# Mixer convolution split by taps, recurrence stages moved back, and new orders at the opening and at four changes of stage, in a two-block float32 transformer kernel

## The chip, the cores and the metric

One core of a Trainium2 chip runs the whole program. The metric is the device time of one execution in microseconds (us); lower is better. Matrix products run on TensorE (PE in the profile), elementwise work on VectorE (DVE) and ScalarE (ACT), loads of weights are issued by SyncE's queue (SP), a few loads and fills by GpSimd (POOL).

## What is computed

A sequence of 256 tokens of width 1024 in float32 goes through two blocks, nine stages in a row (`STAGES`): feed-forward, mixer, feed-forward, twice for the first block, then feed-forward, another mixer, feed-forward for the second.

```python
# first block, for l in range(2): norms modulated by mod = silu(c) @ ada_w + ada_b
x = x + 0.5*mod * swiglu(h)          # 1024 -> 2816 -> 1024
x = x + mod * mixer(h)               # dilated attention and a gated convolution
x = x + 0.5*mod * swiglu(h)
# second block
h = h + 0.5 * rms_norm(swiglu(rms_norm(h)))
h = h + rms_norm(mixer2(rms_norm(h)))
h = h + 0.5 * rms_norm(swiglu(rms_norm(h)))
# in mixer2:
xr = causal_conv(xr, conv_w, conv_b)                 # 4 taps
r, ig = sigmoid(xr @ wa + ba), sigmoid(xr @ wx + bx) # block-diagonal
a = exp(-8 * r * softplus(-lam)); u = sqrt(-expm1(2*log a)) * (ig * xr)
h_t = a_t * h_(t-1) + u_t                            # the recurrence
y_a = (h * gelu(xg)) @ w_lru_out                     # beside windowed attention y_b
```

## The kernel before

**Products.** Each float32 product is made of three: operands are split into a rounded high part and the rest (low). ScalarE writes the high part (`split`, L697, 1.9 us for a 1 MB unit of weights), VectorE subtracts for the low part (`split`, L1170, 2.29 us, or `low_part`, L1177, by halves), and TensorE does low x high, high x low, high x high (`mm3` L1774 to L1776, `tok3` L1781 to L1783). SyncE loads the units in the order of use into three slots `raw`; the load of unit n waits until the low part of unit n-3 is done. High and low parts have three slots more, and every fourth unit of a feed-forward goes to a fourth one (`w3`).

**Orders by hand.** Each engine has a program of its own, written in the order in which it shall work, with semaphores between them. An instruction that waits holds everything behind it on its engine.

**Opening.** Eight units of `ada_w` (named u0 to u7 here) make the scales and shifts of the first norm. TensorE takes u1, u3 and u6 (`ada_cols_of`, L2040), VectorE u0, u2, u4, u5 and u7 in this order (`ada_unit`, L1193 and L1196), each followed on TensorE by a sum over partitions (L2055). When all are done, VectorE's `mods` (L1214, L1217) makes gain and shift. The norm of a tile of 128 tokens is: sums of squares on ScalarE (`norm_x`, L715 to L727), `normed` on VectorE (L1247), eight transposes on TensorE (`turn_x`, L1852), then `apply` on ScalarE (L762, L768) and VectorE (`lows`, L1272; in the second tile also L1258, L1260). In the opening, tile 0 is normed just before u7 and turned before `ada_cols_of(6)`. Tile 1 is normed after the second unit's low part and turned in the midst of the first product, by `mid` in `up(0, 1, 0, s, ...)`.

**Feed-forward.** Eleven groups i: two units of gate and up weights (`up`), transposes of the hidden tile (`turn_h`, L1870), then the down product of the group before (`down`), whose operands are `cH` (ScalarE, `hidden`, L853) and `cL` (VectorE, `low`, L1394). On VectorE the order in group 1 is: one unit of `ada_w` where this stage has one (4.2 us), low part of unit 5, `low(0)`, low part of unit 6. At the start both engines split unit 3 and then do `silu` (L844, L847) and `mult` (L1387, L1390) of group 0.

**Changes.** Between stages `change` computes statistics, the residual and the next norm. After stages 5 and 7 (`BARE`) the transposes take `x` itself and the factor of the norm is applied later, in `silu` and `mult`; ScalarE's order is there: apply, split of unit 2, `next_stats` of both tiles, load of the Silu table. After stage 6 ScalarE does: statistics of the product for tile 0, the first half of them for tile 1 (`row_first`), statistics of the new `x` for tile 0, the second half for tile 1. `squared` counts these for VectorE.

**Second mixer (stage 7).** TensorE works in 28 half units hu of 24 products (0.12 us apart each). After two of three comes one `tick` of attention (scores L1936, transposes L1947, product with the values L1962), after the third nothing; in the middle of the third `chunk_T` (L1974) turns a pair of heads. Six half units, hu - 2 = 6j + i, serve chunk j of the recurrence: unit "c" (convolution input), "q" (queries), "g" (gate). VectorE does `conv2(j)` at i = 0: copy L1714, then four taps (L1720 once, L1727 three times, each in two halves), and only then the next tick's logits (L1456, L1459) and `otok` (L1477) of the tick before. ScalarE does exponentials in each tick (L902), and around them sigmoids (L1100, L1102), tanh and exp (L1110, L1111), sqrt (L1114), `gelu` (L1121) and the high part `cH` (L1117), changing its activation table whenever the set differs. VectorE's stages of `lru(j, k)`: k = 0 at i = 4, k = 1 at i = 5, k = 2 (product, scan L1699, product with gelu) at i = 1 of the next chunk, k = 3 (`cL`, L1707) at i = 2. TensorE's products of the gates (L2174, L2176) come after the tick at i = 2 and wait for all taps. The units after these, `tail`, end in the output projection; its first recurrent unit waits at L1774 for the last `cL`.

## Time and profile before

| what | value |
|---|---|
| median of 3 runs | 2119.05 us (2118.66 to 2120.47) |
| the profiled execution | 2119.83 us, span 2118.0 us |
| PE busy | 2065.3 us, 98% of the span |
| DVE busy | 1419.6 us, 67% |
| ACT busy | 1031.6 us, 49% |
| granted TensorE clock | 0.996 on average |
| chain that ended last | PE 84%, DVE 6%, ACT 5%, DMA 2%, issue 2% |

The profiled execution's own time is 1.8 us above its span, and 0.8 us above the median. TensorE is nearly always busy; each gap in its work is shown in the trace with the engine and the line that ended it.

### The profile page before, as it was taken

The numbers are of one execution on the slowest core, as the hardware profiler recorded it, in microseconds if no ns is written. First come the engines' busy times: TensorE is split into PE (matmuls) and PEld (weight loads), VectorE is DVE, ScalarE is ACT, GpSimd is POOL, SyncE is SP. The second block draws the span as 40 slices with busy tenths as digits, with TensorE's granted clock in tenths as the row PEclk, the third lists the DMA queues.
The fourth block names the chain that finished last, engine by engine and source line by source line (L and its number), as shares of the span: only waits on it lengthen the run. The fifth ranks groups of instructions, "written<-read, shape, count | busy, mean of one in ns | idle before, by whom it ended". The sixth has DMA issues, their size and how long they took to land.

```text
span 2118.0 us, 29720 instructions
## 1 busy us (share of the span) xinstructions
PE 2065.3 (98%) x12033; PEld 1811.1 (86%) x12033; DVE 1419.6 (67%) x1801; ACT 1031.6 (49%) x1278; POOL 36.5 (2%) x78
## 2 busy tenths in 40 slices
PE   6999999999999999999999999999999899899998
PEld 6788899999888878888999998887788788897887
DVE  5787677668777777767766786555555577656454
ACT  3543544444544363445454446444644569646443
POOL 0000000000000000000000000000000000000000
PEclk9999999999999999999999999999999999999999
DMA  9787698547687758758865585554656434456552
GB/s 298 251 272 250 199 298 253 130 133 253 229 267 251 249 170 285 243 195 270 280 173 142 176 291 194 194 179 150 227 180 195 131 126 134 158 181 203 187 196 80
DMA packets 355933, 438.11 MB, mean 207 GB/s; under 512 B 9571, under 2 KB 323371, under 8 KB 355796
## 3 DMA queue, kind: packets, MB, share of 16 engines
q1 hardware_dynamic: 350592, 420.51, 60.8%
q0 software_dynamic: 4160, 14.23, 3.1%
q8 instruction: 96, 1.57, 0.3%
q10 hardware_dynamic: 1044, 1.46, 0.2%
q14 instruction: 41, 0.34, 0.0%
HBM read 435.05 MB, written 1.11 MB: 206 GB/s over the span
## 4 chain that ended last, share of the span: by engine, by line
PE 84%; DVE 6%; ACT 5%; DMA 2%; issue 2%; DVEq 1%; SPq 0%; ACTq 0%
PE PC L1781 7%; PE PC L1783 7%; PE PC L1782 7%; PE PA L1781 6%; PE PA L1783 6%; PE PA L1782 6%; PE PB L1781 5%; PE PB L1783 5%; PE PB L1782 5%; PE PA L1774 5%; PE PA L1775 5%; PE PA L1776 5%; PE PC L1774 2%; PE PC L1776 2%; PE PC L1775 2%; DVE acc L1196 2%
## 5 line engine op out<-in xcount | busy, mean ns | idle before, releaser
L1170 DVE TENSOR_TENSOR lo<-raw,hi 128x2048 fp32r<-128x2048 f32 x275 | 628.8, 2289 | 229.7 <-ACT hi L697 229.1
L697 ACT ACTIVATE hi<-raw 128x2048 fp32r<-128x2048 f32 x277 | 529.0, 1911 | 264.0 <-PE PC L1783 130.3
L1774 PE MATMUL PA<-nl,hi 128*128 128x256 f32 x976 | 281.5, 288 | 1.0 <-ACT f L1090 0.9
L1775 PE MATMUL PA<-nh,lo 128*128 128x256 f32 x976 | 276.0, 283 | 0.0
L1776 PE MATMUL PA<-nh,hi 128*128 128x256 f32 x976 | 275.9, 283 | 0.0
L1196 DVE SCALAR_TENSOR_TENSOR acc<-raw,cs,acc 128x256 f32<-128x256 f32 x448 | 217.1, 485 | 34.0 <-issue 0.4
L1781 PE MATMUL PA<-hi,nl 128*128 128x512 f32 (+1 forms) x528 | 210.8, 399 | 10.7 <-DVE nl L1272 7.6
L1783 PE MATMUL PA<-hi,nh 128*128 128x512 f32 (+1 forms) x528 | 206.4, 391 | 0.0
L1782 PE MATMUL PA<-lo,nh 128*128 128x512 f32 (+1 forms) x528 | 205.9, 390 | 0.0
L1774 PEld LDWEIGHTS PA<-nl,hi 128*128 128x128 f32 x976 | 187.0, 192 | 2.8 <-issue 1.1
L1775 PEld LDWEIGHTS PA<-nh,lo 128*128 128x128 f32 x976 | 187.0, 192 | 0.3
L1776 PEld LDWEIGHTS PA<-nh,hi 128*128 128x128 f32 x976 | 186.9, 191 | 0.0
L1781 PE MATMUL PB<-hi,nl 128*128 128x512 f32 x400 | 157.5, 394 | 0.6 <-DVE nl L1272 0.6
L1783 PE MATMUL PB<-hi,nh 128*128 128x512 f32 x400 | 156.0, 390 | 0.0
L1782 PE MATMUL PB<-lo,nh 128*128 128x512 f32 x400 | 155.6, 389 | 0.0
L1170 DVE TENSOR_TENSOR w<-raw,w 128x2048 fp32r<-128x2048 f32 x51 | 116.8, 2289 | 55.6 <-ACT w L697 55.6
L1781 PE MATMUL PC<-hi,cL 128*128 128x512 f32 x384 | 151.2, 394 | 2.6 <-DVE cL L1394 2.6
L1783 PE MATMUL PC<-hi,cH 128*128 128x512 f32 x384 | 149.7, 390 | 0.0
L1782 PE MATMUL PC<-lo,cH 128*128 128x512 f32 x384 | 149.5, 389 | 0.0
L1781 PEld LDWEIGHTS PA<-hi,nl 128*128 128x128 f32 x528 | 100.8, 191 | 34.2 <-issue 9.3
L1783 PEld LDWEIGHTS PA<-hi,nh 128*128 128x128 f32 x528 | 100.9, 191 | 20.9
L697 ACT ACTIVATE w<-raw 128x2048 fp32r<-128x2048 f32 x51 | 97.4, 1910 | 43.3 <-PE PC L1783 43.3
(305 smaller groups left out, 3867.2 us busy)
## 6 DMA issues: line engine op xcount, KB each, us to landing
raw<-in_w_in SPq DMA_DIRECT2D x90, 1024.0 KB, 6.4
raw<-in_ada_w SPq DMA_DIRECT2D x66, 1024.0 KB, 7.2
raw<-in_ffn_w_gate SPq DMA_DIRECT2D x88, 512.0 KB, 4.1
raw<-in_ffn_w_up SPq DMA_DIRECT2D x88, 512.0 KB, 5.1
raw<-in_ffn_w_down SPq DMA_DIRECT2D x44, 1024.0 KB, 5.0
raw<-in_ffn_w SPq DMA_DIRECT2D x88, 512.0 KB, 4.8
raw<-in_ffn_w SPq DMA_DIRECT2D x22, 1024.0 KB, 4.9
raw<-in_w_o SPq DMA_DIRECT2D x12, 1024.0 KB, 6.3
```

The costliest lines, as they stand in the source:

```text
L697: A(parts_of(n)[0], raw[:, n % 3, :], ACT.Copy).then_inc(hi_done, 1)
L1170: V.tensor_tensor(l, raw[:, n % 3, :], h.bitcast(F32), ALU.subtract).then_inc(lo_done, 1)
L1196: i = V.scalar_tensor_tensor(o, w[:, k, :], cs[:, k:k + 1], o, ALU.mult, ALU.add)
L1774: MM(o, wh[:, c0:c0 + w], xl, start=first, stop=False, skip_group_check=True)
L1775: MM(o, wl[:, c0:c0 + w], xh, start=False, stop=False, skip_group_check=True)
L1776: return MM(o, wh[:, c0:c0 + w], xh, start=False, stop=last, skip_group_check=True)
L1781: MM(o, xl, wh[:, c0:c0 + w], start=first, stop=False, skip_group_check=True)
L1782: MM(o, xh, wl[:, c0:c0 + w], start=False, stop=False, skip_group_check=True)
L1783: return MM(o, xh, wh[:, c0:c0 + w], start=False, stop=last, skip_group_check=True)
```

## The change

The diff, with its context cut. In the opening, VectorE norms tile 0 ahead of u5 and tile 1 ahead of `mods`; TensorE turns tile 0 and takes u6 before the sum of u5, and turns tile 1 after the last sum, so that `mid` is gone there. In group 1 of each feed-forward `low(0)` goes ahead of the low part of unit 5. After stages 5 and 7 the split of unit 3 goes ahead of the statistics on ScalarE and ahead of the reciprocals on VectorE. After stage 6 the statistics of tile 0's new `x` go ahead of both halves of tile 1's. In stage 7 taps 2 and 3 go behind the next tick (i = 1), `lru` stage 2 from i = 1 to i = 2, stage 3 from i = 2 to i = 4, ScalarE's `gelu` from i = 4 to i = 5 and its high part `cH` from i = 1 to i = 3. No instruction that computes is added or taken out.

```diff
...
 
 def squared(s, t, h):
 
-    if (s, t) == (6, 1):
-        return 3 * STAT[("p", 6, 0)] + 3 + (6 if h else 1)
     return 3 * STAT[("p", s, t)] + (3 if h else 1)
 
 
...
                     final_stats(1)
                     apply(Aq, 1)
                     split(BASE[s + 1] + 2)
+                    split(BASE[s + 1] + 3)
                     next_stats(s, 0)
                     next_stats(s, 1)
                     A(spare[:, :], eps[:, 0:1], ACT.Silu)
                 elif s == 6:
                     row_std(*post_of(s, 0))
-                    row_first(*post_of(s, 1))
                     next_stats(s, 0)
-                    row_second(*post_of(s, 1))
+                    row_std(*post_of(s, 1))
                     apply(Aq, 0)
                     next_stats(s, 1)
                     apply(Aq, 1)
...
                     row_std(*post_of(s, 1))
                     apply(Aq, 1)
                     split(BASE[s + 1] + 2)
+                    split(BASE[s + 1] + 3)
                     next_stats(s, 0)
                     next_stats(s, 1)
                     A(spare[:, :], eps[:, 0:1], ACT.Silu)
...
                     act.wait_ge(hT_done, (fo * NG + i) * 2 + t + 1)
                     A(by_tile(hid(cH, i))[:, t], turned(i)[:, t], ACT.Copy).then_inc(hH_done, 1)
 
-                split(b + 3)
+                if s - 1 not in BARE:
+                    split(b + 3)
                 silu(0, 0)
                 silu(0, 1)
                 split(b + 4)
...
 
                 act.wait_ge(rg_mm, j + 1)
                 if j:
-                    act.wait_ge(lru_v, 6 * j)
+                    act.wait_ge(lru_v, 6 * j - 1)
                 for m in range(2):
                     c = 2 * j + m
                     A(ra[:, m * T:(m + 1) * T], RA[:, m * T:(m + 1) * T], ACT.Sigmoid,
...
                     tick(2, 32, 0, t, STEPS)
                 if c is not None:
                     chunk_T(8 + c, c, oH2)
+                if i == 5 and 0 <= j < 4:
+                    gelu(j)
                 if i == 3 and j >= 0:
                     recurrent_gates(j)
+                if i == 3 and 1 <= j < 4:
+                    lru(j - 1, 2)
                 if i == 0 and j >= 1:
                     lru(j - 1, 1)
                 if i == 4 and 0 <= j < 4:
                     lru(j, 0)
-                    gelu(j)
                 if hu % 2 == 0 and u >= 0:
                     after(b + 3 + u)
                     if SPREAD[u] == "q":
...
                     elif SPREAD[u] in ("ga", "gc"):
                         gate2(f1 if SPREAD[u] == "ga" else f2, SPREAD[u], 0, prod[1])
                     split(b + 6 + u)
-                if i == 1 and j >= 1:
+                if i == 1 and j == 4:
                     lru(j - 1, 2)
 
             def last_chunks():
...
                     final_norm(1)
                     apply(Aq, 1)
                     behind()
+                    split(BASE[s + 1] + 3)
                     recip(("n", Aq, 0))
                     recip(("n", Aq, 1))
                 elif s == 6:
...
                     add_postnorm(s, 1)
                     apply(Aq, 1)
                     behind()
+                    split(BASE[s + 1] + 3)
                     recip(("n", Aq, 0))
                     recip(("n", Aq, 1))
                 else:
...
                     V.tensor_tensor(by_tile(hid(cL, i))[:, t], turned(i)[:, t], by_tile(hid(cH, i))[:, t].bitcast(F32),
                                     ALU.subtract).then_inc(hL_done, 1)
 
-                split(b + 3)
+                if s - 1 not in BARE:
+                    split(b + 3)
                 mult(0, 0)
                 mult(0, 1)
                 split(b + 4)
...
                 for i in range(1, NG - 1):
                     if i > 1 or first is None:
                         ada(mid[i])
-                    split(b + 3 * i + 2)
+                    if i > 1:
+                        split(b + 3 * i + 2)
                     low(i - 1)
+                    if i == 1:
+                        split(b + 3 * i + 2)
                     if i == 1 and first is not None:
                         ada(mid[i])
                     split(b + 3 * i + 3)
...
                 if n == 2:
                     dve.wait_ge(rowsT, 1)
                     V.tensor_copy(vec[:, :], PA[:, 0:384]).then_inc(vec_done, 1)
-                if n == 4:
+                if n == 3:
                     normed(0, 0)
                 dve.wait_ge(raw_full[u] if u < 4 else ada_in[u - 4], 16)
                 ada_unit(u * UC, first_ada(u), ada_d)
+            normed(0, 1)
             mods(0)
             low_part(0, 0)
             lows(0, 0, (0, 1))
             low_part(0, 1)
             lows(0, 0, (2, 3))
             split(1)
-            normed(0, 1)
+            dve.drain()
             apply(0, 1)
             split(2)
 
...
                     V.tensor_scalar(xc[:, m * T:(m + 1) * T], cpad[:, m, 1:1 + T],
                                     vec[:, V_CONV2 + c:V_CONV2 + c + 1], vec[:, V_CONVB2 + c:V_CONVB2 + c + 1],
                                     ALU.mult, ALU.add)
-                for tap in (1, 2, 3):
+                taps2(j, (1,))
+
+            def taps2(j, taps):
+
+                for tap in taps:
                     dve.drain()
                     for m in range(2):
                         c = V_CONV2 + 8 * tap + 2 * j + m
                         i = V.scalar_tensor_tensor(xc[:, m * T:(m + 1) * T], cpad[:, m, 1 + tap:1 + tap + T],
                                                    vec[:, c:c + 1], xc[:, m * T:(m + 1) * T], ALU.mult, ALU.add)
-                i.then_inc(xc_done, 1)
+                if taps[-1] == 3:
+                    i.then_inc(xc_done, 1)
 
             for hu in range(2 * len(SPREAD)):
                 t, c, u = tick_of(hu), chunk_of(hu), (hu - 3) // 2
...
                     tick(2, 32, 0, t, 8, STEPS)
                 if i == 0 and 0 <= j < 4:
                     conv2(j, c)
+                if i == 1 and 0 <= j < 4:
+                    taps2(j, (2, 3))
+                if i == 4 and 1 <= j < 4:
+                    lru(j - 1, 3)
+                    dve.drain()
                 if i == 4 and 0 <= j < 4:
                     lru(j, 0)
                 if i == 5 and 0 <= j < 4:
                     lru(j, 1)
-                if i == 1 and j >= 1:
+                if i == 2 and 1 <= j < 4 or i == 1 and j == 4:
                     lru(j - 1, 2)
                 if i == 0 and j == 4 and c is not None:
                     chunk_T(8 + c, c, oH2, oL2)
...
                     split(b + 6 + u)
                 if i == 3 and c is not None:
                     chunk_T(8 + c, c, oH2, oL2)
-                if i == 2 and 1 <= j < 4:
-                    lru(j - 1, 3)
 
             def last_chunks():
                 split(b + 19)
...
                         m.then_inc(d_done, 1)
 
                 up(0, 0, 0, s)
-                up(0, 1, 0, s, lambda: turn_x(s, 1))
+                up(0, 1, 0, s, (lambda: turn_x(s, 1)) if s else None)
                 up(0, 0, 1, s)
                 up(0, 1, 1, s)
                 if first is not None:
...
                     rows_turned()
                 if n == 1:
                     ada_cols_of(3)
-                if n == 4:
+                if n == 3:
                     turn_x(0, 0)
                     ada_cols_of(6)
                 pe.wait_ge(ada_d, n + 1)
                 for c in (2 * u, 2 * u + 1):
                     i = MM(MOD[:, c:c + 1], acc[:, c * P:(c + 1) * P], ones[:, 0:1], start=True, stop=True)
             i.then_inc(mod_done, 1)
+            turn_x(0, 1)
 
             def bias_lines():
```

## Rows read from the trace of the kernel before

**Rows 1.** The page, its first line

```profile
span 2118.0 us, 29720 instructions
```

**Rows 2.** Timeline of PE, 0 to 62 us: start us, us, instruction, [idle before <-releaser]

```profile
31.66 1.01 PE L2055 MATMUL PB<-ones,acc 128*128 128x1 f32 x4 [3.58 <-DVE acc L1196]
32.54 1.95 PE L1852 MATMUL PC<-ident,xn_b 128*128 128x128 f32 x8
34.28 6.83 PE L2040 MATMUL PB<-cs,early 128*128 128x1 f32 x32
...
44.59 0.76 PE L1781 MATMUL PA<-hi,nl 128*128 128x512 f32 x1 [2.63 <-DVE nl L1272]
...
50.97 0.55 PE L1781 MATMUL PA<-hi,nl 128*128 128x512 f32 x1 [1.85 <-DVE lo L1170]
...
53.45 1.65 PE L1852 MATMUL PC<-ident,xn_b 128*128 128x128 f32 x8
54.85 0.48 PE L1781 MATMUL PA<-hi,nl 128*128 128x512 f32 x1
```

**Rows 3.** Timeline of DVE, 0 to 62 us

```profile
26.93 0.35 DVE L1193 TENSOR_SCALAR acc<-early,cs 128x256 f32<-128x256 f32 x1
...
31.76 0.88 DVE L1247 TENSOR_SCALAR xn_b<-x,rstd 128x512 f32<-128x512 f32 x2
32.56 0.35 DVE L1193 TENSOR_SCALAR acc<-early,cs 128x256 f32<-128x256 f32 x1
...
42.00 0.17 DVE L1214 TENSOR_TENSOR modt<-PB,vec 128x16 f32<-128x16 f32 x1 [5.17 <-PE PB L2055]
```

**Rows 4.** Waits of PE, whole span: us in total, times, longest us

```profile
PE PA L1870 <- DVE f L1387: 2.7, 2, 1.3
...
PE PC L1781 <- DVE cL L1394: 2.6, 2, 1.3
```

**Rows 5.** Timeline of DVE, 575 to 605 us (stage 2, group 1)

```profile
594.55 2.28 DVE L1170 TENSOR_TENSOR lo<-raw,hi 128x2048 fp32r<-128x2048 f32 x1
596.75 0.68 DVE L1394 TENSOR_TENSOR cL<-PA,cH 128x512 fp32r<-128x512 f32 x1
```

**Rows 6.** Waits of PE, 1669 to 1845 us (change after stage 6, then stage 7)

```profile
PE PC L1974 <- DVE otok L1477: 4.9, 3, 1.6
...
PE PC L1852 <- DVE xn_a L1247: 2.4, 1, 2.4
PE PB L1947 <- ACT S L902: 2.2, 3, 0.7
PE PC L1936 <- DVE negm L1459: 1.7, 3, 0.6
PE PA L1774 <- DVE cL L1707: 1.3, 1, 1.3
PE PC L1962 <- DVE oL L1484: 0.9, 1, 0.9
PE PA L1774 <- ACT f L1090: 0.9, 1, 0.9
PE PA L1774 <- DVE oL L1484: 0.6, 1, 0.6
```

**Rows 7.** Timeline of ACT, 1655 to 1690 us

```profile
1666.23 0.61 ACT L715 ACTIVATE f<-x 128x512 f32<-128x512 f32 x1
```

**Rows 8.** Windows: PE, PEld, DVE, ACT, POOL busy, granted clock, DMA share, GB/s

```profile
1669.00:1673.00 4.00, 1.84 (x8) 1.44 (x8) 3.83 (x9) 2.49 (x8) 0.41 (x1) 0.52 0.00 0
```

**Rows 9.** Timeline of DVE, 1730 to 1762 us (stage 7, j = 1)

```profile
1736.79 2.79 DVE L1727 SCALAR_TENSOR_TENSOR acc<-cpad,vec,acc 128x256 f32<-128x256 f32 x6
...
1741.73 1.27 DVE L1699 TENSOR_TENSOR_SCAN acc<-acc 128x256 f32<-128x256 f32 x2
```

**Rows 10.** Timeline of ACT, 1690 to 1840 us (stage 7)

```profile
1732.77 1.28 ACT L902 ACT_TABLE_LOAD   x1
...
1838.42 1.92 ACT L697 ACTIVATE hi<-raw 128x2048 fp32r<-128x2048 f32 x1 [5.16 <-PE PA L1776]
```

## The prediction, before the changed kernel had run

> **What bounds the kernel now.** I read the page first: the span is 2118.0 us [rows 1], and the chain that ended last runs mostly through TensorE. So I went to the waits of PE, and for each wait to the timelines of PE, DVE and ACT around it. All its waits together are some 45 us, in a few places, and this change touches most of those places. Nothing of the arithmetic changes, so the gain can only be idle time of TensorE that goes, or time at its half clock. The sum is made against the profiled execution's own 2119.83 us (span 2118.0 and 1.8 around it), 0.78 above the median of 2119.05; I take the same difference from the median. About 0.2% (4.2 us) is what a measurement of this kernel can tell from no change.
>
> **Opening.** TensorE stands still 3.58 us up to 31.66, waiting for VectorE's u5, and only then turns tile 0 (32.54 to 34.28) and takes u6 (6.83 us) [rows 2]. VectorE's `mods` at 42.00 waits for the sums behind it [rows 3]. With the change tile 0 is normed when u4 ends, at 26.93, for 1.05 us (0.88 and a reciprocal) [rows 3]; TensorE, free at 31.66 - 3.58 = 28.1, turns it (1.74 us, to 29.8), takes u6 (to 36.5) and does the two sums (about 1 us each by the row at 31.66, pipelined 1.9, to 38.4). VectorE, later by the norm, ends u5 at 28.0 + 4.6 = 32.6 (26.93 to some 31.5 before) and u7 4.3 later, at 36.9 [rows 3], before the sums need them. `mods` then starts at 38.4 in place of 42.0: 3.6 us less. All that follows up to the first product at 44.59 [rows 2] moves with it. Norming tile 1 (1.05 us) fits on VectorE between 36.9 and 38.4. Turning tile 1 moves out of the first product, where it took 53.45 to 54.85, 1.4 us [rows 2], into the gap of 2.6 us before that product. The wait of 1.85 us for the low part of unit 1 [rows 2] stays, since its chain (apply, split, low part) is unchanged. On the other side, the products at 50.97 to 53.45 are 0.42 us apart against 0.23 later [rows 2]: after that wait the array is at half clock, and the turning covered part of it. Now three more products fall into it, 0.6 us. Opening: 3.6 + 1.4 - 0.6 = **4.4 us**. Whether u6 has landed by 29.8 no row shows; u7, behind it on the queue, was there at 32.56 [rows 3]. So the bounds are 4.4 - 2.7 = 1.7 and, without the clock's part, 5.0 and a little more; I take 4.4 because the loads follow each other and u6 must be some 3 us before u7. The later stretch (units 2 to 5 and their refills) moves as a whole; a unit is refilled when its low part is done, which is earlier too.
>
> **Group 1 of the feed-forwards.** TensorE waited 1.3 us twice for `cL` [rows 4], in stages 2 and 3, where a unit of `ada_w` stands ahead on VectorE. The 2.28 us low part of unit 5 lay between that unit and `low(0)` [rows 5]. Swapped, `cL` is ready at 594.55 + 0.7 = 595.3, and TensorE comes at 596.3: both waits go, **2.6 us**. Unit 5's low part ends 0.7 us later, and so does the load that takes its slot; TensorE needs unit 5 only after four down products of 1.35 us each, and low part of unit 6 and `mult` keep their time. Zero for the other four stages, where no wait stands; cover lost there would cost at most those 0.7 us each.
>
> **Unit 3 after stages 5 and 7.** TensorE waited 1.3 us twice for `mult` (f, L1387) [rows 4]; VectorE did a low part of 2.29 us there while the hidden tile was due, because ScalarE split unit 3 only after its statistics and the table. Moved ahead, ScalarE's total before `silu` is the same, but VectorE's low part falls beside the statistics, where it was idle. Both waits go: **2.6 us**. What could be late is unit 3's load, with the statistics queued behind it; loads there are issued one after another and were no wait before. Then the next to be late is `low(0)`, which the swap of group 1 takes care of: 2.3 us earlier. Bounds 1.3 and 2.7.
>
> **After stage 6.** Statistics of the new `x` started at 1666.23 [rows 7], behind the first half of tile 1's, which itself waited for TensorE's last products but one. `x` is ready at about 1664.6. So they start 1.6 us earlier, and so do `normed`, the turning that waited 2.4 us [rows 6], the second tile's residual and the first `nl`. VectorE's product for tile 1 needs ScalarE's squares, now about 1668.4, as late as its own turn comes. **1.6 us**. The granted clock is 0.52 from 1669 to 1673 [rows 8], right after that wait, and TensorE's next products run at it. I leave this as it is; bounds 0.5 (the squares come late) and 3.2 (the clock stays up, see the rivals).
>
> **Stage 7.** Three chunks lose 1.7 + 2.2 + 4.9 = 8.8 us, 2.9 each: 0.56 for logits, 0.73 for exponentials, 1.63 for `otok` [rows 6]. Logits stood behind four taps; two of them, four of the six instructions of 2.79 us [rows 9], 1.86 us, go behind the tick. That is over three times the wait of 0.56. Exponentials stood behind a table load of 1.28 us [rows 10] that gelu had forced; with gelu behind the tick's exponentials that load is not needed, one per chunk, and 0.73 goes too. `otok` of the next tick stood behind product, scan (1.27 us) [rows 9] and product, 2.7 us in all; they leave and 1.86 of taps come in, while TensorE also arrives 1.3 earlier. Walking VectorE's queue through chunk 1, with its low part before the convolution 0.7 us earlier because ScalarE's split no longer waits for gelu, `otok` is ready 4.9 us after TensorE starts the tick and needed after 5.0. TensorE's gate products need all taps 1.8 us after that start, and get them 1.2 us earlier. In chunk 2 ScalarE has 22.3 us of work from one long exponential to the next short one, which leaves 0.3 to 0.4 us of wait. So some 0.8 of 8.8 stays: **8.0 us**.
>
> The tail gives some back. VectorE's `cL` of chunk 2 now stands before the first step of chunk 3 (0.68 us by the same shape in [rows 5], with its drain 0.75). From there ScalarE works without a gap to its idle of 5.16 us before 1838.42 [rows 10], so everything to the last `cL` is 0.75 later. Of the four waits 0.9, 0.9, 0.6 and 1.3 [rows 6] the gate's and the chunk's 0.6 go, one 0.9 stays, and the last becomes 1.3 + 0.75 + 0.6 = 2.6 us. Together 3.7 become 3.5: **0.2 us**. And a wait of 2.6 us is as long as the one before the half clock of [rows 8]. In [rows 2] 1.85 us was enough; the slow stretch there, 50.97 to 54.85, cost 6 x 0.2 and 0.6 for the turning, 1.8 us. Nearest to these rows, I take a fall: **minus 1.7 us**, bounds 0 and 3.4.
>
> The Trainium skill (ScalarE: Activation LUTs, section What ACT_TABLE_LOAD costs) puts a switch of table at 2.66 us with its drain. Here the exponential starts 1.29 us after the load; with the page's figure a chunk would free 2.66 us on ScalarE, and the sum would be the same, for the wait is gone with 1.28.
>
> **Sum:** 4.4 + 2.6 + 2.6 + 1.6 + 8.0 + 0.2 - 1.7 = 17.7 us. 2119.83 - 17.7 = 2102.1 for a profiled execution, 2119.05 - 17.7 = **2101.3 us** for the median.
>
> **Rivals.**
> (A) The clock holds in both places. After stage 6 the two waits are shorter, and after the tail 2.6 us is borderline. For it: gaps of 1.6 us in stage 7 left the clock at full. Against: [rows 8]. It gives 1.7 for the tail and up to 1.6 after stage 6, where the first product group ran at half: 2098.0. The Trainium skill (TensorE: Matmul & The Clock Gate, HAM oscillation) says that waits inside a product stream make the clock fall again and again; this trace agrees in two places.
> (B) In stage 7 the taps take the recurrence's place. If ScalarE's splits come as late as before, VectorE's queue ends as late, and the `otok` wait of 1.6 stays three times: 2101.3 + 4.9 = 2106.2. For it: VectorE and ScalarE both had little idle in that stretch; against: 2.7 us leave and 1.86 come.
> (C) u6 lands late, up to 2.7 us: 2104.0.
> (D) The waits only move: each engine's order is new, but the next wait takes the whole. It gives 2119; against it speak the margins found above (1.0 us for `cL` in group 1, 1.2 us for the taps).
> (E) Slower: the half clock, once there after the longer tail wait, stays through the output projection and the change, from 1836 to 1943. 107 us of work at half would cost up to 107 us more (2208); it decides from 17.7 us lost, which is 18 us of full-clock work done at half. To be slower by over 4.2 it needs 22 us. A fall held for long is in no row; the fall at 1669 was over by 1680.
>
> **Numbers.** Forecast 0.55, A 0.2, B 0.12, C 0.08, D 0.03, E 0.02. The first four are faster by over 0.2%: 0.95; same 0.03; slower 0.02. Range: B and C together with a low bound after stage 6 give 2108; A with the full opening and 9.5 us in stage 7 gives 2095.5. So 2095.5 to 2108.
>
> **What would show it.** In the profile after: `mods` at about 38.4 and no turning in the first product; no wait for `cL` L1394 and none for `f` L1387; turning after stage 6 with a wait of 0.8 in place of 2.4; waits for logits and exponentials nearly gone in stage 7, three table loads fewer; the last `cL` wait grown to 2.6 us. It would be wrong if the `otok` waits stay, if u6 shows a DMA wait, or if a long stretch at half clock stands after the tail.

## The result, and the profile after

| | before | after |
|---|---|---|
| median | 2119.21 us (2118.66 to 2120.47) | 2100.54 us (2097.93 to 2103.07) |
| ratio to before | 1 | 0.9911, 95% interval 0.9894 to 0.9928 |
| profiled execution | 2119.83 us | 2100.8 us |

The change takes 18.7 us off the median, where 17.7 were forecast. Before was run once more beside it, so its median here is over four runs and 0.16 above that of the first table. The page after, its first line, the busy times and the chain that ended last:

```profile
span 2098.9 us, 29721 instructions
...
PE 2062.8 (98%) x12033; PEld 1810.4 (86%) x12033; DVE 1419.4 (68%) x1801; ACT 1027.4 (49%) x1275; POOL 36.4 (2%) x78
...
PE 84%; DVE 7%; ACT 4%; DMA 3%; issue 1%; DVEq 1%; SPq 0%; ACTq 0%
```

TensorE works 2.5 us less than before with the same 12033 products, so nearly all of the gain is idle time that went. To see where, I set the start of each product against that of the same product before; where the difference grows the change gains, where it shrinks something is given back. These are two single executions, 19.1 us apart in their spans.

| stretch | before / after, start of the same product | gain there | forecast |
|---|---|---|---|
| opening, up to | 67.69 / 62.91 | +4.78 | +4.4 |
| up to stage 2, three small losses | 574.99 / 571.18 | -0.97 | 0 |
| stage 2, group 1 | 614.49 / 609.49 | +1.47 - 0.28 | +1.3 |
| stage 3, group 1 | 808.22 / 803.29 | +1.40 - 1.47 | +1.3 |
| stage 4 | 1047.02 / 1043.27 | -1.18 | 0 |
| after stages 5 and 7 | 1497.49 / 1492.21 and 1943.45 / 1924.56 | +1.79, +1.75 | +2.6 |
| after stage 6 | 1681.69 / 1673.47 | +1.49 + 1.19 | +1.6 |
| stage 7 and its tail | 1830.79 / 1813.40 | +9.17 | +8.0 + 0.2 - 1.7 |
| sum | | +19.14 | +17.7 |

The total is close because errors of both signs cancel: group 1 and stage 4 brought 2.7 us less than forecast and three small places 1.0 less, while the opening brought 0.4 more and everything from stage 5 on 4.7 more. Part of that is small and regular: a wait of 1.31 us that goes moves the next product by 1.47, and one of 1.62 moves it by 1.78. The 512-column products here are listed 0.39 us long and start 0.23 apart, so the first one behind a wait starts some 0.16 later than the idle time in brackets tells.

**Opening.** The timeline of PE after, 27 to 50 us (start us, us, instruction, [idle before <-releaser]), which answers to [rows 2]:

```profile
28.23 1.95 PE L1870 MATMUL PC<-ident,xn_b 128*128 128x128 f32 x8
29.97 6.83 PE L2058 MATMUL PB<-cs,early 128*128 128x1 f32 x32
36.66 1.84 PE L2073 MATMUL PB<-ones,acc 128*128 128x1 f32 x8
38.37 1.95 PE L1870 MATMUL PC<-ident,xn_b 128*128 128x128 f32 x8
...
47.51 0.50 PE L1799 MATMUL PA<-hi,nl 128*128 128x512 f32 x1 [1.21 <-DVE lo L1173]
```

and of DVE, which answers to [rows 3]:

```profile
27.09 0.88 DVE L1250 TENSOR_SCALAR xn_b<-x,rstd 128x512 f32<-128x512 f32 x2
...
38.54 0.17 DVE L1217 TENSOR_TENSOR modt<-PB,vec 128x16 f32<-128x16 f32 x1 [0.76 <-PE PB L2073]
```

The reader is to see that no line of PE from 28 to 38 has an idle time in brackets: u6 had landed, and the stall of 3.58 us is gone. `mods` starts at 38.54, 3.5 us earlier. The windows (us, then busy us and instructions of PE, PEld, DVE, ACT, POOL, granted clock, DMA share, GB/s) show the clock, after:

```profile
60.00:63.00 3.00, 3.00 (x9) 2.33 (x8) 2.73 (x8) 1.91 (x1) 0.29 (x1) 0.52 1.12 361
```

and before:

```profile
51.00:55.00 4.00, 4.00 (x15) 3.36 (x16) 0.88 (x2) 0.46 (x2) 0.00 (x0) 0.57 1.02 369
60.00:63.00 3.00, 3.00 (x14) 1.86 (x13) 2.09 (x1) 3.00 (x4) 0.00 (x0) 1.00 0.00 0
```

The half clock (1.2 GHz) that stood at 51 us before stands at 60 after. The difference of the starts is 6.35 us from 52 to 59 (times of after) and falls to 4.78 in that late stretch, which so takes back 1.6 us. Swap alone and `gelu` alone (below) keep the opening of before, have no slow stretch there, and stand 1.5 ahead of before at 75 us; opening alone has none either, and stands 6.1 ahead. So the new opening is worth 4.6 us with the stretch on neither side and 4.7 with one on both: the extra 0.6 that I had charged for the clock is not there.

**Waits of TensorE after, whole span** (engine, what waits, releaser: us in total, times, longest), which answer to [rows 4]:

```profile
PE PB L2058 <- DMA raw<-in_ada_w: 8.5, 2, 6.8
PE PA L1799 <- DVE nl L1275: 7.1, 8, 3.2
...
PE PC L1799 <- DVE cL L1399: 1.6, 2, 1.4
PE PA L1792 <- DVE cL L1717: 1.2, 1, 1.2
```

No wait for `mult` (f L1387 before) is among the long ones any more. One for `cL` stays at 1.41 us, in stage 3. It is a later one than before, as the timelines of PE and DVE after, 780 to 805 us, show:

```profile
803.29 0.47 PE L1799 MATMUL PC<-w,cL 128*128 128x512 f32 x1 [1.41 <-DVE cL L1399]
```

```profile
796.07 0.35 DVE L1196 TENSOR_SCALAR acc<-raw,cs 128x256 f32<-128x256 f32 x1 [4.74 <-DMA raw<-in_ada_w]
```

The row of DVE before that answers to it:

```profile
798.98 0.35 DVE L1193 TENSOR_SCALAR acc<-raw,cs 128x256 f32<-128x256 f32 x1 [2.72 <-DMA raw<-in_ada_w]
```

VectorE stands 4.74 us for a unit of `ada_w`, 2.72 before, and `cL` is behind it. SyncE's queue issued that load behind unit 8 (gate weights, then up), after:

```profile
786.30 0.37 SPq L507 DMA_DIRECT2D raw<-in_ffn_w_gate  x1
...
787.26 0.51 SPq L527 DMA_DIRECT2D raw<-in_ada_w  x1
```

and before:

```profile
790.62 0.37 SPq L509 DMA_DIRECT2D raw<-in_ffn_w_gate  x1
...
791.58 0.51 SPq L529 DMA_DIRECT2D raw<-in_ada_w  x1
```

TensorE was 5.0 us ahead of before when the stage came, 6.4 after its first wait had gone; the load is 4.3 ahead. Against the 5.0 it is 0.7 us late, just what the swap delays the low part of unit 5 whose slot unit 8 takes, and against the 6.4 it is 2.1 us. It is also used 8.8 us after its issue (796.07 - 787.26) where before it was 7.4. That longer time counts as much as the order: before, `cL` was ready 2.2 us ahead of TensorE; 1.4 of these went with TensorE's gain at the first wait, 0.7 with the later issue and 1.4 with the longer load, and without the last the wait of 1.41 would be under 0.1. Four traces of this study have the swap and this load in its old place in the queue: it takes 8.7 to 9.2 us there, and 7.4 to 7.9 in seven of the eight without the swap (8.7 in the eighth, recurrence alone). In stage 2 it takes 7.5 to 7.7 with the swap too. Why it takes longer is open.

**After stage 6.** The timeline of PE after, 1661 to 1674 us:

```profile
1661.99 1.09 PE L1870 MATMUL PC<-ident,xn_a 128*128 128x128 f32 x8 [0.89 <-DVE xn_a L1250]
...
1666.26 0.36 PE L1799 MATMUL PA<-hi,nl 128*128 128x256 f32 x1 [3.18 <-DVE nl L1275]
...
1673.47 0.36 PE L1799 MATMUL PA<-hi,nl 128*128 128x256 f32 x1 [1.67 <-DVE nl L1275]
```

and its window, as [rows 8]:

```profile
1666.00:1673.00 7.00, 5.55 (x32) 5.33 (x32) 3.47 (x12) 4.05 (x13) 0.12 (x1) 0.76 0.21 77
```

The turning waits 0.89 in place of 2.4. The clock still falls, but for less of the stretch, and that gives 1.19 us more. This part is not the change's: opening alone, which leaves the order after stage 6 as it was, gains 1.21 us at the same place, mixer alone 0.8, and the other kernels of this study between 0.1 and 1.2 whichever order they have. The profiled execution of before has the longest stretch at half clock of them all here.

**Stage 7.** Waits of PE after, 1661 to 1826 us, which answer to [rows 6] (the two for `nl` among them stand ahead of the stage):

```profile
PE PA L1799 <- DVE nl L1275: 4.8, 2, 3.2
PE PA L1792 <- DVE lo L1173: 1.4, 1, 1.4
PE PA L1792 <- DVE cL L1717: 1.2, 1, 1.2
PE PC L1980 <- DVE oL L1493: 0.9, 1, 0.9
PE PC L1870 <- DVE xn_a L1250: 0.9, 1, 0.9
PE PA L1792 <- ACT f L1090: 0.5, 1, 0.5
PE PB L1965 <- ACT S L902: 0.2, 1, 0.2
```

All of the waits for `otok` (4.9 us) and `negm` (1.7) are gone, and of those for S 0.2 is left. In the tail I had forecast one wait of 2.6 us for the last `cL`. It came as two, after:

```profile
1813.40 0.38 PE L1792 MATMUL PA<-cL,hi 128*128 128x256 f32 x1 [1.43 <-DVE lo L1173]
1817.05 0.39 PE L1792 MATMUL PA<-cL,hi 128*128 128x256 f32 x1 [1.24 <-DVE cL L1717]
```

The size is right (2.67), the shape is not, and the window behind them shows no fall:

```profile
1812.00:1819.00 7.00, 4.35 (x34) 4.15 (x35) 6.25 (x5) 3.87 (x3) 0.00 (x0) 1.00 0.61 192
```

### The profile page after: what moved, and what is told of

The parts are those of the page before. It is cut to its first block, busy times and chain, and to the rows that moved or that the text cites. A ratio compares the mean times of both kernels' runs of the same rounds, so it can differ in the third digit from the quotient of the medians.

```text
span 2098.9 us, 29721 instructions
## 1 busy us (share of the span) xinstructions
PE 2062.8 (98%) x12033; PEld 1810.4 (86%) x12033; DVE 1419.4 (68%) x1801; ACT 1027.4 (49%) x1275; POOL 36.4 (2%) x78
## 4 chain that ended last, share of the span: by engine, by line
PE 84%; DVE 7%; ACT 4%; DMA 3%; issue 1%; DVEq 1%; SPq 0%; ACTq 0%
PE PC L1799 7%; PE PC L1801 6%; PE PC L1800 6%; PE PA L1799 6%; PE PA L1801 6%; PE PA L1800 6%; PE PB L1799 6%; PE PB L1801 6%; PE PB L1800 6%; PE PA L1792 5%; PE PA L1793 5%; PE PA L1794 5%; PE PC L1792 2%; DMA raw<-in_ada_w 2%; PE PC L1794 2%; PE PC L1793 2%
```

## The experiments

The changed kernel ran again, and eleven variants. Ratios are to before, in runs on the same chip; the medians of before were 2119.8, 2119.63 and 2119.57 us. "Offset" is the difference of starts of the same product.

### The changed kernel again

Unaltered, to see which of the small gains and losses recur.

> The changed kernel again, unaltered. Theory: its time is some 2100.5 us (ratio 0.991), and the two waits that the kernel before did not have, 1.4 us for cL in stage 3 and 1.2 us for a low part in stage 4, come from transfers of ada_w that land later; if they hang on the order of the work they are there again, within 0.3 us. Rival: they are chance of the transfers, and are gone or elsewhere in this trace, with the span shorter by as much (up to 2.6 us). The same for the clock: the half-clock stretch around 60 to 63 us may be elsewhere.

Measured: 2100.91 us, ratio 0.9908 (0.9892 to 0.9924). The wait in stage 3 recurs:

```profile
802.75 0.47 PE L1799 MATMUL PC<-w,cL 128*128 128x512 f32 x1 [1.30 <-DVE cL L1399]
```

The one of stage 4 does not. The stretch at half clock in the opening stands elsewhere than in the first trace of the same kernel, by its windows:

```profile
47.00:50.00 3.00, 2.68 (x7) 2.15 (x8) 2.81 (x9) 1.39 (x4) 0.00 (x0) 0.61 1.02 344
60.00:63.00 3.00, 3.00 (x14) 2.40 (x14) 3.00 (x4) 1.92 (x1) 0.00 (x0) 1.00 1.00 314
```

So the 1.2 us of stage 4, and the place of the slow stretch in the opening, belong to an execution and not to the change; stage 3's loss belongs to the change.

### The parts alone: opening, mixer, swap

Opening: only the new places of `normed`, `turn_x` and the end of `mid`.

```diff
-                if n == 4:
+                if n == 3:
                     normed(0, 0)
...
+            normed(0, 1)
             mods(0)
```

> The kernel before with the opening's edits alone (tile 0 normed ahead of u5, tile 1 ahead of mods, turned after the last sum). Theory: mods 3.5 us earlier and 1.4 us of turning out of the first product, less or more what the half clock takes: 4 to 6 us, 2114.5 us. Rival: the gain of the opening is mostly the clock's chance, and the kernel is only 3 us faster, 2116.

Measured: 2115.28 us, ratio 0.998 (0.9971 to 0.999). That is 4.5 us under before, by the ratio 4.2 (2.1 to 6.1). The forecast of 4.4 stands. Its trace is 6.1 us ahead after the opening; 1.5 of that is the slow stretch that before has there and this execution has not, and 1.8 is lost again to a wait in stage 4.

Mixer: all edits of stage 7, nothing else.

```diff
+                if i == 1 and 0 <= j < 4:
+                    taps2(j, (2, 3))
...
-                if i == 1 and j >= 1:
+                if i == 2 and 1 <= j < 4 or i == 1 and j == 4:
                     lru(j - 1, 2)
```

> The kernel before with stage 7's edits alone. Theory: the three chunks lose their 8.8 us of waits, the tail gains 0.7 and gives back 0.8 and more at the last cL, in all 9.2 us as in the changed kernel: 2110 us. Rival: part of the 9.2 came from the clock or from the shorter way into the stage; then 7 us or less, 2112 or more.

Measured: 2111.81 us, ratio 0.996 (0.9945 to 0.9975): 8.5 us by the ratio, 8.0 by the medians. Within stage 7 its offset goes from -3.57 to +5.65, 9.2 us, as in the changed kernel. Its waits there, 1690 to 1845 us, are all in the tail:

```profile
PE PA L1785 <- DVE lo L1173: 1.4, 1, 1.4
PE PA L1785 <- DVE cL L1710: 1.2, 1, 1.2
...
PE PA L1785 <- ACT f L1090: 0.5, 1, 0.5
```

Swap: `low(0)` ahead of the low part of unit 5, nothing else.

```diff
-                    split(b + 3 * i + 2)
+                    if i > 1:
+                        split(b + 3 * i + 2)
                     low(i - 1)
+                    if i == 1:
+                        split(b + 3 * i + 2)
```

> The kernel before with the swap of group 1 alone (low(0) ahead of the low part of unit 5). Theory: 1.3 us won in stages 2 and 3, and given back in part because unit 5's low part, and with it the refill of its slot and the ada_w unit behind it on SyncE's queue, is 0.7 us later: stage 3 shows a new wait of about 1.4 us for cL of group 1, net 1 us or less, 2118 to 2119 us. Rival: the new wait belongs to the shift of the whole program against the transfers, and is not there; then 2.6 us won, 2116.5.

Measured: 2119.06 us, ratio 0.9994 (0.9985 to 1.0004). The offset gains 1.5 us at 597.58 and as much at 791.34, and loses 0.3 in stage 2, 1.4 at 808.22 in stage 3 and 1.2 in stage 4. Stages 2 and 3 make 1.2 us net, near what was expected, and too little for the median to show. The loss in stage 4 is no part of the swap: such a wait comes and goes between executions (above).

### Stage 7 taken apart

Three kernels, each with one of the mixer's three moves.

Taps alone: the recurrence and `gelu` stay, taps 2 and 3 go behind the tick.

```diff
-                for tap in (1, 2, 3):
+                taps2(j, (1,))
...
+                if i == 1 and 0 <= j < 4:
+                    taps2(j, (2, 3))
```

> The kernel before, with taps 2 and 3 of stage 7's convolution behind the next tick and nothing else moved. Theory (each edit takes one wait; queues decide): the logits' wait of 0.56 goes, but the exponentials still stand behind gelu's table load, so that wait grows from 0.73 to 1.3, and otok stands behind the same sum of work on VectorE, so its wait stays at 1.6: no gain, 2119.5 us, within 0.5. Rival: the split itself is what won the 9 us; then at least 3 us faster.

`gelu` alone, on ScalarE:

```diff
+                if i == 5 and 0 <= j < 4:
+                    gelu(j)
...
                     lru(j, 0)
-                    gelu(j)
```

> The kernel before, with only gelu moved behind the next tick's exponentials. Theory: three table loads fewer (ACT count of L902 loads 9 to 6), ScalarE's split 1.3 us and VectorE's whole queue 0.66 us earlier: the waits for logits and exponentials go, otok's grows from 1.6 to 2.3; 0.65 per chunk and 0 to 0.6 in the tail, 2 to 2.5 us faster, 2117.5. Rival: ScalarE is off the path, and nothing is won: 2119.5.

Recurrence alone: `lru` stages 2 and 3 later, with ScalarE's `cH` and its wait to match; the four taps stay together.

```diff
+                if i == 4 and 1 <= j < 4:
+                    lru(j - 1, 3)
+                    dve.drain()
...
-                if i == 1 and j >= 1:
+                if i == 2 and 1 <= j < 4 or i == 1 and j == 4:
                     lru(j - 1, 2)
```

> The kernel before, with only the recurrence's stages 2 and 3 moved back (and the high part on ScalarE with them). Theory: 2.7 us leave VectorE's queue ahead of otok, so its wait of 1.6 goes three times; logits and exponentials keep 0.56 and 0.73; the tail's last cL is 0.75 later: 4 to 4.5 us faster, 2115.5. Rival: the recurrence was hidden, and without the split of the taps it only moves the wait: under 1 us.

Measured:

| kernel | median us | ratio, interval | waits for negm, S, otok in the three chunks |
|---|---|---|---|
| before (beside the three parts) | 2119.63 | | 1.7, 2.2, 4.9: 8.8 us |
| taps alone | 2120.82 | 1.0002 (0.9993 to 1.0011) | 0, 4.1, 5.0: 9.1 us |
| gelu alone | 2119.26 | 0.9993 (0.9984 to 1.0003) | 0, 0, 6.5: 6.5 us |
| recurrence alone | 2114.9 | 0.9971 (0.996 to 0.9982) | 1.7, 2.2, 0: 3.9 us |
| all three moves (before 2119.8) | 2111.81 | 0.996 (0.9945 to 0.9975) | 0, 0, 0 |

Their rows in the waits of PE, 1690 to 1845 us, taps alone:

```profile
PE PC L1981 <- DVE otok L1477: 5.0, 3, 1.7
PE PB L1954 <- ACT S L902: 4.1, 3, 1.4
```

gelu alone:

```profile
PE PC L1975 <- DVE otok L1478: 6.5, 3, 2.2
```

recurrence alone:

```profile
PE PB L1950 <- ACT S L902: 2.2, 3, 0.7
PE PC L1939 <- DVE negm L1461: 1.7, 3, 0.6
```

The three waits stand one behind another in each chunk. Logits that come earlier only make TensorE wait for the exponentials, which are still behind the table load (0.7 grew to 1.4 each). Moving `gelu` takes that load away: in 1720 to 1815 us before, and in 1715 to 1815 with gelu alone, ScalarE's loads at this line (busy us, mean ns, idle ahead) are

```profile
L902 ACT ACT_TABLE_LOAD x9 | 11.5, 1283 | 0.2
```

```profile
L902 ACT ACT_TABLE_LOAD x6 | 7.7, 1283 | 0.1
```

and TensorE then comes sooner to `otok`, which VectorE's queue has not made any earlier (1.6 grew to 2.2). Only the recurrence, the last in the row, gives time on its own: 5.7 us in stage 7 by the offset. The parts do not add up to the 9.2 of all together; the other two become worth their waits when the last is gone.

With gelu alone I expected 2 to 2.5 us. The median is 0.4 lower, and the interval (3.4 us faster to 0.6 slower) neither shows that gain nor rules it out. In the trace the offset gains 0.9 us per chunk, 2.7 in all, and falls again behind two of the three longer waits, by 1.5 each. The timeline of PE and the window behind one of them:

```profile
1745.07 0.48 PE L1975 MATMUL PC<-ident,otok 128*128 128x128 f32 x2 [2.15 <-DVE otok L1478]
```

```profile
1746.00:1748.00 2.00, 2.00 (x11) 2.00 (x11) 0.17 (x1) 2.00 (x3) 0.00 (x0) 0.50 1.08 371
```

The granted clock is half (1.2 GHz) there. The waits of 1.6 us of [rows 6] had left it up. That the longer wait is the cause is likely but not shown: the third wait, 2.16 us at 1805.00, has no fall behind it, and in opening alone, whose stage 7 is that of before, the clock falls behind waits of 0.55 and 0.74 us, by its timeline of PE and its window:

```profile
1736.99 0.44 PE L1948 MATMUL PB<-ident,S 128*128 128x128 f32 x2 [0.74 <-ACT S L902]
```

```profile
1738.00:1741.00 3.00, 3.00 (x10) 2.46 (x10) 2.93 (x4) 0.90 (x2) 0.00 (x0) 0.50 0.02 5
```

Swap alone has such a fall at 1800. Neither of the two cost anything: TensorE came later to `otok`, the wait of 1.6 us for it was not there, and the offset behind it is what it was (4.91 and 4.92).

### Unit 3 and the order after stage 6, without the swap

Only the early splits of unit 3 after stages 5 and 7, and the new order of statistics after stage 6.

```diff
                     split(BASE[s + 1] + 2)
+                    split(BASE[s + 1] + 3)
                     next_stats(s, 0)
...
-                if (s, t) == (6, 1):
-                    return 3 * STAT[("p", 6, 0)] + 3 + (6 if h else 1)
```

> The kernel before, with unit 3 split ahead of the statistics after stages 5 and 7, and the new order of statistics after stage 6. Theory: 1.3 us twice and 1.5 us once, and up to 1.2 more where the clock comes back sooner after stage 6; in group 1 of stages 6 and 8, without the swap, cL may be 0.3 late: 4 to 5.5 us faster, 2115 us. Rival: in those two stages the wait only moves from mult to cL, and 2 us are won, 2117.5.

Measured: 2117.54 us, ratio 0.9989 (0.9979 to 0.9998), 2.1 us by the medians. The gain of 1.5 us at 1497 is lost again at 1503.65: the wait has moved to `cL` of group 1, of which there are now four, as its row in the waits of PE shows:

```profile
PE PC L1784 <- DVE cL L1396: 4.5, 4, 1.4
```

After stage 6 it gains 1.5, and 0.1 by the clock in place of 1.2. In stage 8 1.5 comes and 0.5 goes.

### The changed kernel without the swap

The changed kernel with `split(b + 5)` back in front of `low(0)`, in all six stages.

> The changed kernel without the swap of group 1. Theory: the swap pays 1.3 us in each of stages 6 and 8, where unit 3's early split needs it, and next to nothing in stages 2 and 3 (1.3 + 1.3 less 1.4 and 0.3): cL waits of 1.3 in stages 2 and 3 and up to 1.3 in 6 and 8; 2.5 to 3.5 us slower than the changed kernel, 2103.7 us. Rival: in the changed kernel the swap is worth what it is worth alone, about 1 us: 2101.8.

Measured: 2104.64 us, ratio 0.9923 (0.9909 to 0.9937): 3.7 us above the changed kernel's 2100.91, although the swap alone had shown nothing in the median. The intervals of the two ratios overlap, so here too the traces decide. The waits for `cL` are four again:

```profile
PE PC L1796 <- DVE cL L1399: 4.1, 4, 1.4
```

Against the changed kernel's trace it loses 1.25 us at 1498, 0.7 at 1930, and 1.1 in stages 2 and 3 together (1.5 twice, less 0.4 and 1.6). A wait of 2.08 us in stage 4 with a fall of the clock behind it stands in this profile too. As stage 4's wait comes and goes between executions of one kernel, I don't count it: for the swap that makes 3.0 us, 2 of them in stages 6 and 8.

### The wait of stage 3

The load of the unit of `ada_w` for group 2 goes ahead of unit 8's on SyncE's queue, in stages after the first.

```diff
                 for i in range(NG - 2):
+                    if i == 1 and s:
+                        load_ada(mid[i + 1])
                     up(i + 2, 0)
-                    if i:
+                    if i > 1 or i and not s:
                         load_ada(mid[i + 1])
```

> The changed kernel, with the load of ada_w for group 2 of stages 2 and 3 issued ahead of unit 8's load, which waits for unit 5's low part. Theory: the wait of 1.4 us for cL in stage 3 stands because the swap delays that low part by 0.7 us and with it the ada_w load behind it on SyncE's queue; issued some 3 us earlier it lands in time: the wait in stage 3 (and 0.24 in stage 2) goes, 1.5 us faster, 2099.2 us. Rival: the transfers' rate and not the issue sets the landing; the wait stays, or moves to unit 8's low part.

Measured: 2098.75 us, ratio 0.9896 (0.9882 to 0.991). The interval overlaps the changed kernel's, so the trace decides. The unit is there when VectorE comes, with no idle time before it:

```profile
790.68 0.34 DVE L1198 TENSOR_SCALAR acc<-raw,cs 128x256 f32<-128x256 f32 x1
```

TensorE's wait at this place is gone: 1.6 us against the changed kernel in stage 3 and 0.5 in stage 2. The load, issued at 782.93, has landed by 788.01. So the loss of stage 3 is this load, issued behind a delayed one and slow in coming, as the queue's rows suggested.

### The tail

The changed kernel with `cL` of chunk 2 at i = 3 of chunk 3, ahead of `lru(3, 0)`'s group, and `gelu(3)` ahead of its tick.

```diff
                     A(gl, prod[(1, 0, 1, 0)[j]], ACT.Copy).then_inc(gc_done, 1)
+                    if j == 3:
+                        gelu(j)
...
+                if i == 3 and j == 3:
+                    lru(j - 1, 3)
+                    dve.drain()
```

> The changed kernel, with two orders of stage 7's last chunk altered: VectorE's cL of chunk 2 goes behind chunk_T at i = 3 (into an idle time of 0.8 us) in place of ahead of chunk 3's first step, and ScalarE's gelu of chunk 3 goes ahead of its tick (into its idle times of 0.8 and 1.4 us). Theory: the 0.75 given back and gelu's 1.9 leave ScalarE's unbroken chain to the last cL; the two waits before it, 1.4 and 1.2 us, fall to 0 to 0.4 in sum: 2.3 to 2.7 us faster than the changed kernel, 2098 us. Rival: ScalarE's chain is not what sets the last cL, VectorE's low parts are; then under 1 us.

Measured: 2095.91 us (2095.71 to 2100.73), ratio 0.989 (0.9874 to 0.9906). The offset against the changed kernel grows by 2.5 us in the tail, and of the 2.67 us of waits before the last `cL` 0.5 is left:

```profile
PE PA L1797 <- DVE cL L1719: 0.5, 1, 0.5
```

So the tail's last waits come from the order in the last chunk, and can be had back without touching the other three. The median is 4.6 us under the changed kernel's, more than this edit gives: the two profiled executions also differ by 1.6 us in the opening, where this one has no slow stretch, and by 1.4 in stage 4, where it has no wait.

### All three repairs

Both edits above, and in the first block's mixers (stages 1 and 4) VectorE's seventh unit of `ada_w` one place later (n = 12 for 11).

> tail_fix and ada_ahead together, and in stages 1 and 4 VectorE's seventh unit of ada_w one position later (behind the low part at n = 12 in place of n = 11), so that a late landing holds one low part less. Theory: 2.5 + 1.5, and the wait for a low part in stage 4, 0 to 1.2 us and more in the traces so far, gone: 4 to 5.5 us faster than the changed kernel, 2095.5 us. Rival: in stages 1 and 4 the wait only moves to the next unit; 3.5 to 4, 2096.8.

Measured: 2094.91 us (2094.16 to 2096.54), ratio 0.9878 (0.9864 to 0.9892), the lowest median of the study, 5.6 us under the changed kernel's first. In the traces the two repairs give 4.7 us of this: 0.5 in stage 2, 1.6 in stage 3, 2.5 in the tail. Stage 4's wait is absent, but it is absent with either repair alone too. The third edit can't be credited with it.

## Why the prediction was right, and where not

The sign, the size and the place of nearly all of it were right: 18.7 us measured, 17.7 forecast. Point by point:

- **Opening**, 4.4: measured 4.78 in the trace, about 4.2 alone. The part worked out of waits was nearly exact (3.5 for 3.6 at `mods`). The 0.6 for the clock was priced where the slow stretch stood before; it stood elsewhere, and with one such stretch on both sides its net cost is nothing. That before and after each had one is chance: 5 of the 14 traces have none in the opening, two have two, and each is worth 1.5 to 1.6 us. Rival C fell: u6 had landed.
- **Group 1**, 2.6: 1.12. The step that failed is "Unit 5's low part ends 0.7 us later, and so does the load that takes its slot", which I priced by TensorE's need of unit 5 alone. Behind unit 8's load stands that of `ada_w`, VectorE waits for that, and `cL` of the next group is behind it. It gave back 1.4 us in stage 3. The delay of 0.7 alone would not have: the load also took 1.4 us longer, which no row of before could tell. I had counted who waits for the load and not what is queued after it.
- **Unit 3**, 2.6: 3.54. It is worth this only with the swap: the text named `low(0)` as the next to be late, and the two kernels without the swap show it, 1.6 and 1.25 us in stage 6 alone. So 2 of the swap's 3.0 us belong to these two stages, which are among the four where I had put it at zero.
- **After stage 6**, 1.6: 1.49 by the order, and 1.19 by the clock. The first was right and recurs without the other parts (1.5). The second looks like half of rival A and is luck: opening alone got 1.21 with the old order.
- **Stage 7**, 8.0: with the tail 9.17 for 8.2 before the clock's term. I worked out 0.3 to 0.4 us of waits left in chunk 2 and put 0.8 into the sum without a reason for the rest; 0.2 was there. The waits of the chunks give 8.6 us, those of the tail take 0.4 (4.1 for 3.7), which makes 8.2. Of the other 1.0 the nine waits account for 0.8: where they stood the offset grows by 9.4 for 8.6 of idle time. I had priced a wait at its idle time alone. Rival B (the taps take the recurrence's place) fell. That the recurrence leaving VectorE ahead of `otok` is what frees the chunks is shown by its kernel alone.
- **Tail**, +0.2 and -1.7: the wait of 2.6 us was right in sum but came as 1.43 and 1.24, with work between them, and no fall followed, in this trace or in the four others that have both waits. The step that failed is "a wait of 2.6 us is as long as the one before the half clock": I had put at one product what stands at two. That the work between them is why the clock stayed up is argued, not shown. This is rival A's other half. Nor did the gate's wait go, as I had said: 0.5 of its 0.9 stayed.
- **Not in the forecast**: 0.97 us lost in three small places up to stage 2, left open, and 1.18 in stage 4. The latter hangs on when a unit of `ada_w` lands; it is absent or 0.1 us in seven of the 14 traces of this study and 1.2 to 2.6 in the other seven. The unit took 6.3 us from issue to landing in the changed kernel's first trace and 5.1 in its second.
- Rivals D and E: the waits did not only move, although the taps alone show that they can. No long stretch at half clock came.
- **The range**: B and C with the low bound after stage 6 add up to 2101.3 + 4.9 + 2.7 + 1.1 = 2110.0 and not to 2108.
- **Luck**: the total hit within 1 us although neither loss put down for the clock came (0.6 and 1.7 us). Two single executions can differ by several us for no reason in the kernels: a slow stretch in the opening is 1.5, one more or less after stage 6 up to 1.2, stage 4's wait up to 2.6 and up to 3.9 with the fall behind it.

## What to carry to other kernels

Where several waits follow each other in one period of a loop, cost them together: here moving the taps alone gave nothing, gelu alone nothing clear of noise, the recurrence 5.7 us, and all three 9.2. A wait that goes is worth a little more than its idle time (1.47 for 1.31, 1.78 for 1.62 here). Before pricing a delayed instruction at nothing, read on past the load that it frees to what is issued behind that load on its queue, and to who waits for that. A term for the clock, read off one trace, should be held against a second execution first: of the two here neither came. And two waits with products between them are not one wait of their sum.

## What the runs showed of the hardware

- Where TensorE's granted clock falls varies from one execution to the next. None of the 13 waits of 1.6 us for `otok` in the 14 traces had a fall within 3 us behind it, nor had the pairs of 1.43 and 1.24 us with products between them. Single waits of 1.8 to 2.55 us mostly had one, to a granted clock of 0.50 to 0.57 (1.85 us in [rows 2], 2.15 in gelu alone, 2.08 in stage 4 of the kernel without the swap), but 1.81 (stage 3 of the tail's kernel), 1.96 (stage 4 of opening alone) and 2.16 us (gelu alone) had none. Two falls came behind waits of only 0.55 and 0.74 us. So no length of one wait parts the two cases here. I had not expected a fall in stage 7 at all. One cost 1.5 us where TensorE did not wait afterwards, and nothing where a wait of 1.6 us took it up. The Trainium skill (TensorE: Matmul & The Clock Gate, A second HAM failure mode: psum-queue depth-cycling) says that short idle times between groups of products cost throughput by repeated slowing and warming; this trace of gelu alone agrees, with 3.0 us lost over two falls.
- The slow stretch of the opening stood at 60 to 63 us in one execution of the changed kernel and at 47 to 50 in another. Seven of the 14 traces have one between 59 and 69 us with no wait of TensorE over 0.4 us in the 8 us before it.
- The load of a 1 MB unit of `ada_w` in stage 3 was used 7.4 us after its issue before and 8.8 after, VectorE standing idle for it in both; stage 4's wait by such a load varied by over a microsecond from one execution to the next of the same kernel.
